# One step of a hybrid decoder layer on one core: the sample tokens' attention moved to GpSimd and VectorE, and the first norm applied to results

## The reference, cut to what matters

```python
xn = rmsnorm(x, norm_mix)                       # x / rms(x) * gain
lru_x, lru_g, q, k, v = split(xn @ w_in)        # 1024, 1024, 3 x 1536 columns
xc = causal_conv(lru_x, w_conv, b_conv)
hs = rg_lru(xc)                                 # h[t] = a[t] * h[t-1] + u[t]
y_lru = (hs * gelu(lru_g)) @ w_branch_lru
q, k = rmsnorm(q, q_gain), rmsnorm(k, k_gain)   # per head of 64
for g, (window, dil) in enumerate(((128, 1), (512, 4), (2048, 16))):
    outs.append(attention(q[g], k[g], v[g]))    # 8 heads per group
o = combine_groups(outs)                        # weighted by the softmax sums
y_att = o @ w_branch_att
g_lru, g_att = split(sigmoid(xn @ w_merge + b_merge))
x = x + (g_lru * y_lru + g_att * y_att) @ w_o
x = x + (silu(gate) * up) @ w_ffn_out           # of rmsnorm(x, norm_ffn) @ w_ffn_in
```

## Time and profile before

| What | Value |
| --- | --- |
| Median of 3 executions | 2134.76 us (2133.73 to 2136.41) |
| The profiled execution | 2133.12 us, of which the span is 2131.3 us |
| Mean granted clock of TensorE | 0.974 of full speed |
| TensorE, matmuls (PE) | 2051.2 us busy, 96% of the span, 13052 instructions |
| TensorE, weight loads (PEld) | 1994.9 us, 94% |
| VectorE (DVE) | 907.5 us, 43% |
| ScalarE (ACT) | 548.7 us, 26% |
| GpSimd (POOL) | 550.3 us, 26% |
| Moved by DMA | 188.40 MB, 88 GB/s over the span |

### The profile page before, as it was taken

How to read it: one execution, slowest core, us unless ns; L and a number is a source line. 1 busy time by engine, 2 the same in 40 slices (tenths; PEclk the granted TensorE clock), 3 DMA queues, 4 the chain that set the end, 5 groups by cost and what they waited for, 6 DMA issues and landing times.

```text
span 2131.3 us, 33683 instructions
## 1 busy us (share of the span) xinstructions
PE 2051.2 (96%) x13052; PEld 1994.9 (94%) x13052; DVE 907.5 (43%) x1096; ACT 548.7 (26%) x878; POOL 550.3 (26%) x331
## 2 busy tenths in 40 slices
PE   5799899999989999999899999999999999999999
PEld 4799799999979999999899989999999999999999
DVE  8566667677614343323256253433321333213321
ACT  5466634434314443333300011211100011000000
POOL 2222222222211111111112033233233233233232
PEclk9899999999999999999979799999999999999999
DMA  3111112222342423343456162111111111111112
GB/s 127 44 42 42 42 44 87 90 79 90 107 164 94 146 96 140 112 156 107 152 209 236 50 229 89 69 50 39 49 49 40 50 49 39 50 49 40 49 47 92
DMA packets 71404, 188.40 MB, mean 88 GB/s; under 512 B 9258, under 2 KB 28669, under 8 KB 70653
## 3 DMA queue, kind: packets, MB, share of 16 engines
q1 hardware_dynamic: 41392, 136.97, 19.0%
q10 hardware_dynamic: 29964, 50.78, 7.0%
HBM read 145.06 MB, written 45.81 MB: 90 GB/s over the span
## 4 chain that ended last, share of the span: by engine, by line
PE 90%; DVE 4%; DMA 2%; issue 2%; ACT 1%; ACTq 0%; POOL 0%; SPq 0%; DVEq 0%; POOLq 0%
PE ups L466 67%; PE ups L566 12%; PE aux L606 3%; PE ups L585 2%; PE aux L650 1%; PE aux L490 1%; PE aux L628 1%; DMA o_s<-x 1%; PE aux L596 1%; PE aux L517 1%; PE ups L596 1%; DVE ext L1100 1%; DVE big_f L1085 0%; DMA ext<-bt_s 0%; DVE ext L1096 0%
## 5 line engine op out<-in xcount | busy, mean ns | idle before, releaser
L466 PE MATMUL ups<-big,wsp 128*128 128x344 f32 x9360 | 1518.6, 324 | 25.3 <-ACT x L821 5.2
L466 PEld LDWEIGHTS ups<-big,wsp 128*128 128x128 f32 x9360 | 1496.7, 190 | 43.1 <-issue 25.1
L434 POOL CAST wsp<-wraw 128x1024 fp32r<-128x1024 f32 (+2 forms) x160 | 165.2, 1033 | 1526.8 <-issue 696.7
L436 POOL TENSOR_TENSOR wsp<-wraw,wsp 128x1024 fp32r<-128x1024 f32 (+2 forms) x160 | 379.0, 2369 | 12.8
L566 PE MATMUL ups<-big,wsp 128*128 128x344 f32 x1728 | 304.9, 328 | 6.3 <-ACTq L928 6.3
L566 PEld LDWEIGHTS ups<-big,wsp 128*128 128x128 f32 x1728 | 273.5, 190 | 9.7 <-ACTq L928 6.5
L1196 DVE RECIPROCAL x<-x 128x1024 f32<-128x1024 f32 x24 | 157.3, 6553 | 76.2 <-ACT x L887 76.2
L1241 DVE SCALAR_TENSOR_TENSOR x<-ups,ext 128x256 f32<-128x256 f32 (+1 forms) x96 | 52.1, 543 | 206.5 <-PE ups L585 117.5
L1056 ACT ACTIVATE ext<-ext 128x1032 f32<-128x1032 f32 x22 | 23.5, 1067 | 398.9 <-DVE ext L1438 398.9
L1460 DVE TENSOR_TENSOR x<-ups,x 128x1032 f32 x24 | 29.6, 1233 | 213.6 <-PE ups L466 213.6
L1445 DVE TENSOR_TENSOR ext<-ups,ext 128x344 f32<-128x344 f32 x66 | 29.9, 509 | 147.4 <-PE ups L466 147.4
(11 more groups left out here) (192 smaller groups left out, 1229.3 us busy)
## 6 DMA issues: line engine op xcount, KB each, us to landing
wraw<-w_in SPq DMA_DIRECT2D x52, 512.0 KB, 3.4
wraw<-w_ffn_in SPq DMA_DIRECT2D x44, 512.0 KB, 3.2
x<-out_qkv SPq DMA_DIRECT2D x36, 512.0 KB, 4.4
out_qkv<-x ACTq DMA_DIRECT2D x32, 512.0 KB, 3.2
x<-gate_s SPq DMA_DIRECT2D x16, 516.0 KB, 4.2
wraw<-w_merge SPq DMA_DIRECT2D x16, 512.0 KB, 4.8
wraw<-w_ffn_out SPq DMA_DIRECT2D x16, 512.0 KB, 3.5
x<-o_s SPq DMA_DIRECT2D x8, 792.0 KB, 6.5
```

Source lines behind the costliest of these rows:

```text
L434: nc.gpsimd.tensor_copy(hi, raw).then_inc(w_hi, 1)
L436: nc.gpsimd.tensor_tensor(lo, raw, hi.bitcast(F32), ALU.subtract).then_inc(w_split[slot], 1)
L466: ins = nc.tensor.matmul(ups[:, slot, c, 0:CH], wsp[:, slot, w, k, :], src[:, a, k, c * CH:(c + 1) * CH], start=(k == 0 and w + a == 0), s ...
```

## The change

**Sample tokens' attention.** The twelve steps on TensorE in the ylru stage, their steps on VectorE and ScalarE, and SP's six cache loads go. Each group, pair of heads and sample becomes a row, 96 in all (partitions), each of two heads. In the v stage TensorE turns the samples' queries and keys into rows; VectorE and ScalarE norm them there. SP loads the row's 128 keys and 128 values in 16 loads of 96 x 2048, two per iteration of att0 (keys) and att1 (values), and the biases in twelve small copies ahead of att0. GpSimd multiplies (`key_products`, `value_products`), VectorE sums (`key_sums`, `value_sums`), and between the groups come the softmax (`row_softmax`) and the copies for the way back (`row_parts_out`). In the ylru stage TensorE transposes the result once, and VectorE combines the three groups (`row_weights`, `row_output`).

**First norm.** x times gain is split and multiplied without 1/rms; 1/rms (`rrms`, kept until the attention's end) multiplies each result where it leaves PSUM. These multiplications run on VectorE, in place of ScalarE's copies: `first_in`, `branch_in` and `side_in` in the recurrent loop, `tile_in` for queries and keys, `v_in`, and `tile_part` in the attention; the tanh of the merge gates is then one ScalarE pass per tile. The first unit runs k-tile by k-tile as x lands (`by_tiles`), and the sums of squares come while the second unit runs. ScalarE makes the high parts and squares, VectorE the rests.

**Ends of the recurrent loop.** The product with the gelu is left whole in `big2`; its two parts are made by GpSimd in att2 (`z_split_tile`). GpSimd also takes `square_low` over. The first two tiles of the loop are written out on TensorE, and the last two gate chunks stand between the chunks of the first query tile. `stats` follow whole units.

The diff, cut:

```diff
 @block.sync
-            for k in range(KT):
-                sp.dma_start(tmp(k), A["x_T"][k]).then_inc(x_loaded[k], 16)
+            sp.dma_start(gmix[:], A["c_norm_mix"]).then_inc(gm_ld, 16)
...
-                    cache(0)
                     sp.wait_ge(o_stored, O_STORES)
...
                     weights(0, 0)
+                    x_tiles(0, 3)
                     weights(0, 1)
+                    x_tiles(3, KT)
...
+                if name == "att0":
+                    sp.wait_ge(bt_fill, 16)
+                    for g in range(NG):
+                        for f in range(4):
+                            r = 32 * g + NB * f
+                            sp.dma_start(SBI[r:r + NB], ...).then_inc(row_bias, 16)
                 with sp.Fori(first, iters) as i:
                     for slot in range(2):
                         weights(i, slot)
+                    if name in ("att0", "att1"):
+                        for n in range(2):
+                            if name == "att1":
+                                sp.wait_ge(kv_red[n], i + 5)
+                            else:
+                                sp.wait_ge(kv_red[n], i + 1)
+                            src = A["kr" if name == "att0" else "vr"]
+                            sp.dma_start(KVB[n], src[ds(i * 2 + n, 1)]...).then_inc(kv_ld[n], 16)
                     if name.startswith("att"):
...
 @block.gpsimd
+            def key_products(i, n):
+                pool.wait_ge(kv_ld[n], i * 16 + 16)
+                ...
+                nc.gpsimd.tensor_tensor(own, own, q, ALU.mult).then_inc(kv_mul[n], 1)
...
+            def z_split_tile(i, n):
+                ...
+                nc.gpsimd.tensor_copy(hi, z).then_inc(z_hi, 1)
+                ...
+                nc.gpsimd.tensor_tensor(lo, z, hi.bitcast(F32), ALU.subtract).then_inc(z_split, 1)
...
+                if name == "att0":
+                    pool.wait_ge(row_q, 1)
+                if name == "att1":
+                    pool.wait_ge(row_exp, 1)
+                if name == "att2":
+                    pool.wait_ge(lru_done, KT)
+                    pool.wait_ge(row_parts, 1)
...
                 with pool.Fori(first, iters) as i:
                     for slot in range(2):
                         split(name, nk, i, slot)
+                        if name == "qk":
+                            square_low(i - 1, slot)
+                    if name == "att0":
+                        for n in range(2):
+                            key_products(i, n)
+                    if name == "att1":
+                        for n in range(2):
+                            value_products(i, n)
+                    if name == "att2":
+                        for n in range(2):
+                            z_split_tile(i, n)
 @block.tensor
+            def by_tiles():
...
+                for k in range(KT):
+                    pe.wait_ge(xl_done, k + 1)
+                    for c in range(NCH):
...
+            by_tiles()
+            unit("lru", 0, 1, big1, parts=(0, 1))
+            norm_sums()
+            unit("lru", 0, 1, big1, parts=(2,))
+            unit("lru", 1, 0, big1, parts=(0, 1), held=first_evacuated)
+            gates(0, 0)
+            unit("lru", 1, 0, big1, parts=(2,), held=first_evacuated)
+            gates(0, 1)
...
             y_chunks(0, 1)
-            head_squares()
...
+            row_parts_turned()
+            for n, at in enumerate((4, 7, 10, 12, 15, 18, 20, 23)):
+                y_chunks(done, at)
+                turn(n)
+                done = at
+            y_chunks(done, 24)
 @block.scalar
-                act.wait_ge(unit_done[0], i + (T0["lru"] + 2))
-                act.wait_ge(conv_done, i + 1)
-                nc.scalar.activation(chunks(LX[:, 3:3 + NT]), ups_v[0], ACT.Copy).then_inc(ps_free[0], 1)
...
-                nc.scalar.activation(chunks(GE), ups_v[1], ACT.Gelu_apprx_tanh).then_inc(ps_free[1], 1)
+                act.wait_ge(ge_raw, i + 1)
+                nc.scalar.activation(GE, GE, ACT.Gelu_apprx_tanh)
...
+                if g == 1:
+                    act.wait_ge(row_max, 1)
+                    for h in range(2):
+                        ins = nc.scalar.activation(SC[:, h, :], SC[:, h, :], ACT.Exp, bias=..., accum_out=...)
+                    ins.then_inc(row_exp, 1)
 @block.vector
+            def branch_in(i):
+                dve.wait_ge(unit_done[0], i + (T0["lru"] + 2))
+                dve.wait_ge(conv_done, i + 1)
+                nc.vector.tensor_tensor(chunks(LX[:, 3:3 + NT]), ups_v[0], chunks(rrms), ALU.mult).then_inc(ps_free[0], 1)
+            def side_in(i):
+                dve.wait_ge(unit_done[1], i + (T0["lru"] + 2))
+                dve.wait_ge(z_done, i + 1)
+                nc.vector.tensor_tensor(chunks(GE), ups_v[1], chunks(rrms), ALU.mult).then_inc(ge_raw, 1)
+                dve.wait_ge(ge_raw, i + 1)
+                dve.sem_inc(ps_free[1], 1)
...
             with dve.Fori(1, KT) as i:
+                side_in(i - 1)
                 gated(i - 1)
+                branch_in(i)
                 conv(i)
                 recur(i - 1)
...
+            def key_sums(i, n):
+                dve.wait_ge(kv_mul[n], i + 1)
+                ...
+                nc.vector.tensor_reduce(to, KVB[n].rearrange("p (k h e) -> p k h e", k=16, h=2), AX_X, ALU.add).then_inc(kv_red[n], 1)
...
+            def tile_part(g, i, n):
...
+                nc.vector.tensor_tensor(part(GT[j], c), ups[:, 0, c, 0:CH], part(rrms, c), ALU.mult).then_inc(au_ev, 1)
...
+                if g == 1:
+                    row_softmax()
+                if g == 2:
+                    row_parts_out()
                 with dve.Fori(0, 4) as i:
...
+                        if n in (0, 2, 4, 6, 8):
+                            tile_part(g, i, n // 2)
+                    tile_part(g, i, 5)
+                    for n in range(2):
+                        if g == 0:
+                            key_sums(i, n)
+                        if g == 1:
+                            value_sums(i, n)
...
-            tokens(0)
-            s_norm()
...
+            for n in range(8):
+                tokens(n)
+                if n == 0:
+                    row_weights()
+                if n == 2:
+                    row_output()
             split_turned(7)
```

664 lines of the change are left out of this document (318 added, 346 removed).

## The result

The changed kernel takes 2196.5 us (median of 4 runs, 2194.07 to 2198.8) beside 2134.24 us (4 runs of the kernel before on the same chip): a ratio of 1.028, 95% interval 1.0263 to 1.0296. It is 62 us slower; the forecast was 41 slower (2176), range 2120 to 2205. The profiled execution has a span of 2194.8 us against 2131.3, 63.5 more.

What follows compares the result with a forecast made beforehand. The prediction took TensorE as the bound. Terms of -69, -16, +9.5, -4.5, +1.5, +10, +79, +15, +12 and +5 summed to +42.5 us on 2133.1, giving 2175.6, stated as 2176 us, range 2120 to 2205.

Steps and rivals of the forecast that it cites:

- SP held in iterations 1 to 3: Attention groups 0 and 1: V, Q, K and bias queue behind SP's waits for VectorE's sums, scores late: +79 us.
- The clock's share: Same six iterations: after TensorE idles for late loads, a lower granted clock loses some 2.5 to 3 us.
- First iterations: Each attention group's first iteration: bias copies delay group 0's weights, +10 us; GpSimd's row waits delay groups 1, 2: +15, +12.
- GpSimd against VectorE: Attention: GpSimd's products mostly hidden, but small VectorE steps such as the negation sometimes held: +5 us (0 to 20).
- Rival (3): Attention: GpSimd's products block negations in most iterations, 20 us instead of 5, and loads land late: 2205 us; chance 0.12.
- Recurrent loop: Two multiplications by 1/rms lengthen the loop's period to 27.7 us from 26.1, over six iterations: +9.5 us.
- the slack: Recurrent loop: spare time in the chain beside TensorE, taken as the 1.19 us ScalarE's copy waits for TensorE.
- a period of 26.1: Recurrent loop: an unchanged period in us, named beforehand as a sign that the forecast was wrong.
- Front end: Start of the kernel: products start on x without 1/rms, so the second tile's convolution starts earlier: -16 us.
- the rest up to the end of the values: End of the recurrent loop, -4.5 us from earlier statistics; query, key and value work, +1.5 us.
- Output stage: Output of the recurrent branch: sample matmuls and their waits go, some waits stay, leaving 104 us: -69 us.
- Rival (1), SP not held: SP's waits on the sums: loads go out an iteration earlier, the 79 us vanish: 2097 us; chance 0.15.

Runs made afterwards that it cites:

- run 1: Changed kernel with SP's loads of cached rows, and their waits, moved behind V, Q, K and the bias of the same iteration: 2136.3 us.
- run 6: run 5 with the negation of the maximum moved from VectorE to ScalarE: 2096.1 us.
- run 7: run 5, but with the cached rows loaded still later, behind V of the next iteration: 2091.8 us.
- run 8: run 7 with the negation of the maximum moved from VectorE to ScalarE: 2073.0 us.
- run 9: run 8 with the store of an iteration's attention output issued ahead of the last tile's way out on ScalarE: 2048.7 us.
- Run 4: Changed kernel with SP's waits for the sums left ahead of V and only the loads of cached rows moved behind the bias: 2176.8 us.
- run 2: Changed kernel with GpSimd's waits for row data moved from ahead of the attention loops to behind the iteration's weight splits: 2186.6 us.
- run 3: Changed kernel with the twelve copies of bias rows waiting for the short table in DRAM instead of the long one: 2187.6 us.
- run 12: Kernel before the change, with the attention output's store issued first and the negation on ScalarE: 2132.3 us, ratio 0.9976.
- run 11: run 9 without VectorE's combining of the rows in the output stage, sample tokens' attention set to zeros: 2048.6 us.
- run 5: Changed kernel with the three moves of run 1, run 2 and run 3 together: 2113.0 us.

## Why the prediction was right, and where its sum was off

In the profiled execution the sum was 21 us short: 12 in the six iterations, 5 each in group 2 and the output stage, 2 in the first iterations, less 4 up to the end of the values.

**SP held in iterations 1 to 3 (+79 forecast, +91 measured).** Right in place and cause: run 1 gives 59 of the 91 back, and the other 32 are the held negation and the late store, which come up in the same iterations once the scores are early (runs 6 to 9). The order of issues came out as worked out: the two sums took 4.47 us where I took 4.8, and V was issued 6.2 us after the end, 6.1 forecast. Mis-sized is the traffic. I counted 1 us for "0.79 MB of rows more", and two such loads stand ahead of V, 1.5 MB: V landed 8.6 us after its issue (667.08 to 675.68) and the scores ran at 18.1 instead of 15.5. Run 4 shows that traffic without the waits' part, 17.6 us over six iterations. The clock's share was under-counted by a little: TensorE was busy for 4.3 us more than before, where I took 2.5 to 3.

The Trainium skill, "SBUF — State Buffer", section "Summary: rules for kernel authors", has the 358 GB/s by which the prediction put the scores at 16.4, as an estimate. The trace has 18.1: nearer than my 15.5, and still early.

**First iterations (+10, +15, +12; measured +12.1, +14.3, +12.4).** The sums held, by luck in part. For group 1 the step failed that gave the whole to GpSimd's wait, since SP's queue alone costs as much (run 2). For group 2 run 2 confirms the wait, at 8.1 us; the other 4.3 of its 12.4 are what the group's later iterations have as well. For group 0 run 3 confirms the issues ahead of the weights, and shows behind them the stores of the values, which the forecast did not have.

**GpSimd against VectorE (+5, range to 20), and group 2 (nothing of its own).** Measured +9.8 in group 2 alone. Of its 3.3 us an iteration, run 6 shows the held negation (2.7 less) and run 9 the store (34.2 to 32.1 in its later iterations); together more than 3.3, since the kernel before had some of it too (run 12). The late store was in no term: I costed the chunks' move from ScalarE to VectorE, and not the tanh that then stands as one pass of 1.16 us ahead of a store for which VectorE waits. The 5 rested in part on a misreading: the earlier trace rows gives the longest negation, and the trace of the kernel before has it held in every iteration of group 0 (1.04, 1.03, 1.03 and 0.95 us), not once. Rival (3) was right as a mechanism, and the argument against it, that the products would be over before the late scores, held in the kernel after and broke as soon as the scores came early (run 1).

The Trainium skill, "SBUF — State Buffer", section "Who interferes with whom", says that an instruction like the negation can be blocked for the whole of GpSimd's, and that a reduction never is. The runs agree: the negation of 0.17 us took 4.54 beside a product of 4.5, and no reduction between scores and negation was longer than 0.69.

**Recurrent loop (+9.5 forecast, about +3 measured).** The failed step is the slack. I took the 1.19 us that ScalarE's copy waited for TensorE; but a later convolution matters only when the gates wait for it. The timelines, kernel before and kernel after:

```profile
171.94 0.16 DVE L1156 COPY sout<-ext 128x11 f32 x1
...
174.41 1.32 PE L490 MATMUL aux<-x,bd 128*128 128x344 f32 x4
```

```profile
185.67 0.17 DVE L1169 COPY sout<-ext 128x11 f32 x1
...
187.27 1.32 PE L547 MATMUL aux<-x,bd 128*128 128x344 f32 x4
```

Before, the convolution's result was there 2.3 us ahead of TensorE's gates; the two multiplications use up 0.9 of it and TensorE still sets the period of 26.1 us. Only the first and the last of the loop's iterations were longer, by 1.8 and 1.4. The prediction had named a period of 26.1 as a sign against it, and it is what came. This is read from the traces; no run tested it.

**Front end (-16).** The second tile's gates came at 80.97 instead of 96.05, 15.1 earlier. With the loop's 3.2 the rest up to the end of the values, forecast at -3, came to -1.5.

**Output stage (-69, measured -63.6).** Right in kind; the waits were mis-sized. I counted 9 us for them; the idle times above sum to 12.7 (0.66, 2.79, 2.25, 2.46, 1.54, 2.99), and the first chunks ran at a clock of 0.94. I took 1.5 for the first turn, behind the attention's last store; it is this wait, 2.79, that is gone in run 9, whose stage is 104.7. I laid 4 on the new row steps, and run 11 shows some 1 of that: without those steps the wait of 2.25 is gone, but behind the next wait 72 matmuls take 13.1 us instead of 11.6. The prompt's own combines are late at the other turns, with waits of 2.44, 1.55 and 2.99 in run 11 too.

**Rival (1), SP not held,** was priced at 2097. The run nearest to its case is run 1, and it came to 2136: 32 us of the difference stand in the same six iterations, as the negation and the store. So the price of taking SP's wait away was wrong, since these two waits stood behind it unseen; run 5 and run 7, at 2113 and 2092, move other waits as well.

## What to carry to other kernels

A load that waits for a late step takes everything behind it in its queue along; ask of each wait what stands behind it, and put it behind what must not be late. Here one order of issues was worth 60 us, where the change took 42 off TensorE's busy time. Where a wait is removed, the next one on the same path can be nearly as long: in group 1 the queue cost 15 us an iteration, and the store behind it still 7 to 11. Five mends were needed, and the change became a gain of 4.3% only when the last had gone. And a small instruction on the path (the negation of two numbers, the issue of a store) deserves the same question as a large one: which engine's long work lies beside it.

## What was not expected of the hardware

- A VectorE instruction of 169 ns was held for 4.54 us, the full length of a GpSimd product (run 1), while the scores' step (one operand in PSUM) and the reductions beside it were never longer than 0.69.
- With 1.5 MB of rows issued ahead of them, the loads of V, Q and K landed 8.9 us after their issue in the median, against 4.4 before and 4.4 with the rows behind them (run 1); there a store of 0.5 MB from another engine's queue took 11.9 us. The DMA engines' mean share in these stretches was only 0.34 to 0.44.
- After an idle stretch of 16.6 us, 24 matmuls took 6.40 us; after one of 6.3 they took 5.33, and in full flow 3.78. Behind the wait for V, the granted clock was 0.54 of full speed for 10.5 us, near the lower of its two levels (1.2 and 2.4 GHz), and 1.00 in the 29 us that followed, in which TensorE was busy throughout. Over a whole iteration with such a wait it was 0.84 to 0.87, and in a stretch of run 9 without one (840 to 870 us) 1.00.
